# A two-layer decoder trunk on one core: first tile's rows through two PSUM banks, a tile's closing steps moved to later slots, GELU taken of the place matrix

## What is computed

```python
def peer_ffn(xn, w_q, sub_keys, u_tab, v_tab):            # 16384 experts, 8 heads, top 16 of each
    q = (xt @ w_q).reshape(n_tok, 8, 2, 128)
    scores = einsum('thcd,ckd->thck', q, sub_keys)
    top_s, top_i = top_k(scores, 16)                      # then top 16 of the 16 x 16 sums
    gate = softmax(sel_s)                                 # 128 experts and gates for each token
    act = gelu(einsum('td,tkd->tk', xb, u_tab[eb]))
    out = einsum('tk,tkd->td', gb * act, v_tab[eb])
```

## Time and profile before

| | |
|---|---|
| median of 3 executions | 3154.34 us |
| the profiled execution, device time | 3158.17 us |
| its span, first to last instruction | 3156.4 us |
| time outside the span | 1.8 us |
| busy: PE, VectorE, ScalarE, POOL | 2147.1, 2199.8, 1549.0, 1155.9 us |
| mean granted TensorE clock | 0.781 of full |
| DMA | 1185.36 MB, mean 376 GB/s |

### The profile page before, as it was taken

How to read it: one execution, slowest core, us unless ns; L and a number is a source line. 1 busy time by engine, 2 the same in 40 slices (tenths; PEclk the granted TensorE clock), 3 DMA queues, 4 the chain that set the end, 5 groups by cost and what they waited for, 6 DMA issues and landing times.

```text
span 3156.4 us, 40113 instructions
## 1 busy us (share of the span) xinstructions
PE 2147.1 (68%) x13768; PEld 1281.2 (41%) x13768; DVE 2199.8 (70%) x6053; ACT 1549.0 (49%) x3986; POOL 1155.9 (37%) x1041
## 2 busy tenths in 40 slices
PE   7878788674457798777855799878675655453334
PEld 6776454340024475555523466545442312120001
DVE  8646888857776777767676657777866666667663
ACT  3514556443334766775433476787543423343332
POOL 0012344334443333434343433433445444334441
PEclk8889888785567899998876799999886866565555
DMA  6228999999999999979999999998999999999995
GB/s 212 67 86 334 419 419 417 396 369 421 421 420 364 419 404 391 403 287 410 419 420 414 377 356 399 384 388 339 421 420 420 420 421 421 421 419 421 421 421 241
DMA packets 182413, 1185.36 MB, mean 376 GB/s; under 512 B 19648, under 2 KB 25792, under 8 KB 50880
## 3 DMA queue, kind: packets, MB, share of 16 engines
q0 software_dynamic: 147456, 1073.81, 83.0%
q1 hardware_dynamic: 34752, 108.98, 9.1%
HBM read 1180.61 MB, written 2.10 MB: 375 GB/s over the span
## 4 chain that ended last, share of the span: by engine, by line
DMA 37%; PE 31%; ACT 16%; DVE 9%; issue 5%; POOL 2%; another core or an unknown queue 1%; ACTq 0%; SPq 0%; POOLq 0%; DVEq 0%
DMA arena<-uv_tab,cols 37%; PE ps L760 7%; PE xps L696 7%; DVE arena L2179 4%; PE ps L696 4%; POOL arena L653 2%; ACT L1415 2%; ACT scr L1427 2%; ACT cols L1420 2%; PE ps L735 2%; PE xps L1118 2%; PE xps L1192 1%; ACT cols L1415 1%; PE xps L1169 1%; PE xps L1189 1%
## 5 line engine op out<-in xcount | busy, mean ns | idle before, releaser
L653 POOL DMA_INDIRECT arena<-uv_tab,cols x1024 | 1151.7, 1125 | 1944.8 <-PE ps L760 1372.2
L2179 DVE CUSTOM_DVE_ANT_0 arena<-arena 128x1024 f32<-128x1024 f32 x1024 | 1249.8, 1222 | 588.6 <-DMA arena<-uv_tab,cols 558.5
L760 PE MATMUL ps<-arena,scr 128*32 128x512 f32 x4096 | 743.3, 806 | 751.8 <-ACT scr L1427 729.2
L1415 ACT ACTIVATE cols<-cols 128x2 f32<-128x2 f32 x512 | 105.2, 206 | 1008.1 <-DVE cols L2179 998.0
L760 PEld LDWEIGHTS ps<-arena,scr 128*32 128x32 f32 x4096 | 92.7, 123 | 1121.8 <-ACT scr L1427 1036.8
L696 PE MATMUL xps<-arena,wring 128*128 128x256 f32 x1600 | 393.6, 396 | 15.8 <-ACT arena L1628 8.3
L696 PEld LDWEIGHTS xps<-arena,wring 128*128 128x128 f32 x1600 | 304.1, 197 | 105.8 <-issue 43.1
L1427 ACT ACTIVATE scr<-sel,cols 128x32 f32<-128x32 f32 x1024 | 275.3, 316 | 48.4 <-ACT cols L1420 1.9
L696 PE MATMUL ps<-arena,wring 128*128 128x256 f32 x1152 | 292.2, 411 | 6.6 <-DVE arena L1807 4.1
L696 PEld LDWEIGHTS ps<-arena,wring 128*128 128x128 f32 x1152 | 233.7, 207 | 90.7 <-issue 46.2
L1420 ACT ACTIVATE cols<-cols 128x1 f32<-128x1 f32 x1024 | 247.9, 289 | 20.5
(11 more groups left out here) (447 smaller groups left out, 2911.9 us busy)
## 6 DMA issues: line engine op xcount, KB each, us to landing
wring<-wall SPq DMA_DIRECT2D x176, 512.0 KB
arena<-uv_tab,cols POOLq DMA_INDIRECT x1024
arena<-wall SPq DMA_DIRECT2D x16, 512.0 KB, 7.5
h<-xT SPq DMA_DIRECT2D x2, 1024.0 KB, 11.3
arena<-glu_w SPq DMA_DIRECT2D x2, 1024.0 KB, 12.7
out<-arena SPq DMA_DIRECT2D x4, 512.0 KB, 21.0
arena<-s_b SPq DMA_DIRECT2D x1, 512.0 KB, 9.1
arena<-s_bt SPq DMA_DIRECT2D x1, 512.0 KB, 9.8
```

Of the source, the lines that this page charges most:

```text
L653: pool.indirect_dma_start(out=whole_row(at), out_offset=None, in_=uv_tab, in_offset=bass.IndirectOffsetOnAxis(ap=ids[g % 2][:, k:k + 1], a ...
L760: mm = pe.matmul(ps[4 + half][32 * c:32 * c + 32, :], wdiag[:, b % PAIRS, j, :], pair_row(at + j, 1)[:, T * half:T * half + T], start=(g % ...
L1415: mark(act.activation(gelu[g % 2][:, 2 * b:2 * b + 2], dots[g % 2][:, 2 * b:2 * b + 2], ACT.Gelu))
L2179: dve.tensor_tensor_reduce(u, u, xrep[:, block_of(k), :], 1.0, 0.0, ALU.mult, ALU.add, dots[g % 2][:, k:k + 1]).then_inc(s["dot_done"], 1)
```

## The change

Four things are edited.

1. Tile 0's rows have a step of their own, `first_tile_rows`, through banks 0 and 1 in turn in place of the side bank, so PE's step i waits for the copy of step i - 2. PE does six of the eight steps (before: two) ahead of `across(0)`, and ScalarE four of the eight copies (before: two) ahead of `soft(0)`. `u_rows` gets a wait for the last copy, since it writes these banks next. `first_apply(1)` goes from behind dot 0 to behind dot 1.
2. The first round of a later tile: rows 5, 6, 7 go from slots 1, 1.5, 2 to 2, 3.5, 5; the closing steps from 2.5, 3, 4.5 to 6, 7, 8.5 (PE), and from 3, 3.5, 5 to 6.5, 7.5, 9 (ScalarE); `tile_done` from 6 to 9 to 10 to 13; the query of rounds 16, 32 and 48 from 5 to 9.
3. Routing: in these rounds route(r + 2) starts at slot 14 in place of 11, and ScalarE's `soft` of the next head is at slot 5 in place of 3 in the round after.
4. `gelus`: GELU of `place` scaled by the dot (two of 128x32) straight to `wdiag`, then two copies in place scaled by the gate. GELU of a dot into columns, the gate's product there and the spreading go away. The wait for `v_free` moves ahead of the GELU.

```diff
@@ def query_at(gi, q):
-    return 16 * r + (8 if r == 0 else 5 if r % 8 == 0 and r > 0 else 2)
+    return 16 * r + (8 if r == 0 else 9 if r % 8 == 0 and r > 0 else 2)
@@ def rows_at(t, i):
-    return TOPK * PH * t + (-7, -5.5, -4, -2.5, 0.5, 1, 1.5, 2)[i]
+    return TOPK * PH * t + (-7, -5.5, -4, -2.5, 0.5, 2, 3.5, 5)[i]
@@ def side_order():
-    todo = [(-10, "q", 0, -1), (-9, "sc", 0, -1), (-8, "q", 0, -2), (-7.5, "x", 0, 0), (-7.2, "x", 0, 1), (-7, "sc", 0, -2)]
-    todo += [(-6 + 0.1 * i, "x", 0, i) for i in range(2, 8)] + [(4.5, "q", 0, 0), (6.7, "sc", 0, 0)]
+    todo = [(-10, "q", 0, -1), (-9, "sc", 0, -1), (-8, "q", 0, -2), (-7, "sc", 0, -2), (4.5, "q", 0, 0), (6.7, "sc", 0, 0)]
...
-        todo += [(TOPK * (PH * t + 8) + (2.5, 3, 4.5)[i], "hy", t, i) for i in range(3)]
+        todo += [(TOPK * (PH * t + 8) + (6, 7, 8.5)[i], "hy", t, i) for i in range(3)]
@@ PE
+            def first_tile_rows(i):
+
+                pe.wait_ge(s["xn_first"], 1)
+                if i >= 2:
+                    pe.wait_ge(s["rows_done"], i - 1)
+                for k in range(4):
+                    for e in range(4):
+                        mm = pe.matmul(ps[i % 2][32 * e:32 * e + 32, tl(k)], xn[:, 4 * (i % 2) + k, 32 * (i // 2):32 * (i // 2) + 32],
+                                       ident[:, :], start=True, stop=True, skip_group_check=True)
+                mm.then_inc(s["rows_mm"], 1)
...
-            for i in range(2):
-                to_rows(0, i)
+            for i in range(6):
+                first_tile_rows(i)
             across(0)
             first_scores(1)
-            for i in range(2, 8):
-                to_rows(0, i)
+            for i in range(6, 8):
+                first_tile_rows(i)
             first_sum(1)
...
-                    if k in (2.5, 3, 4.5) and done is not None:
-                        finish(done, (2.5, 3, 4.5).index(k))
+                    if k in (6, 7, 8.5) and done is not None:
+                        finish(done, (6, 7, 8.5).index(k))
@@ ScalarE
+            def first_tile_rows(i):
+
+                act.wait_ge(s["rows_mm"], i + 1)
+                act.activation(xrep[:, i // 2, T * (i % 2):T * (i % 2) + T], ps[i % 2][:, :],
+                               ACT.Copy).then_inc(s["rows_done"], 1)
...
-                mark(act.activation(gelu[g % 2][:, 2 * b:2 * b + 2], dots[g % 2][:, 2 * b:2 * b + 2], ACT.Gelu))
+                if 8 * g + b >= PAIRS:
+                    act.wait_ge(s["v_free"], 2 * (8 * g + b - PAIRS) + 2)
                 if b == 0:
                     act.wait_ge(s["gate_found"], g + 1)
+                for n in two:
+                    m = act.activation(wdiag[:, b % PAIRS, n % 2, :], place, ACT.Gelu, scale=dots[g % 2][:, n:n + 1])
+                mark(m)
                 settled()
                 for n in two:
-                    m = act.activation(gelu[g % 2][:, n:n + 1], gelu[g % 2][:, n:n + 1], ACT.Copy,
+                    m = act.activation(wdiag[:, b % PAIRS, n % 2, :], wdiag[:, b % PAIRS, n % 2, :], ACT.Copy,
                                        scale=gate[g % 2][:, n:n + 1])
-                mark(m)
-                if 8 * g + b >= PAIRS:
-                    act.wait_ge(s["v_free"], 2 * (8 * g + b - PAIRS) + 2)
-                settled()
-                for n in two:
-                    m = act.activation(wdiag[:, b % PAIRS, n % 2, :], place, ACT.Copy, scale=gelu[g % 2][:, n:n + 1])
                 m.then_inc(s["w_ready"], 1)
...
-            for i in range(2):
-                to_rows(0, i)
+            for i in range(4):
+                first_tile_rows(i)
             soft(0)
             first_scores(1)
-            for i in range(2, 8):
-                to_rows(0, i)
+            for i in range(4, 8):
+                first_tile_rows(i)
             first_norm(1)
...
-                    if k == 3 and r + 1 < ROUNDS:
+                    if k == (5 if r % PH == 1 else 3) and r + 1 < ROUNDS:
                         soft(r + 1)
...
-                    if k in (3, 3.5, 5) and done is not None:
-                        finish(done, (3, 3.5, 5).index(k))
+                    if k in (6.5, 7.5, 9) and done is not None:
+                        finish(done, (6.5, 7.5, 9).index(k))
@@ VectorE
             def tile_done(t):
-                yield 6
+                yield 10
...
-                    if r == 0 and k == 0:
+                    if r == 0 and k == 1:
                         first_apply(1)
...
-                    if k == (14 if r == 0 else 11 if r % PH == 0 else ROUTE_SLOT):
+                    if k == (14 if r % PH == 0 else ROUTE_SLOT):
                         nxt = route(r + 2) if r + 2 < ROUNDS else iter(())
```

More of the change, by code:

```diff
@@ L514, in trunk @@
         dots = [rcol(384 + 16 * i, TOPK) for i in range(2)]
-        gelu = [rcol(416 + 16 * i, TOPK) for i in range(2)]
         def score_at(t, q):
@@ L531, in trunk @@
             "g_sq", "g_sum", "g_root", "mix1_ready", "out_added", "hsq_ready", "hsum", "h_root", "xn_ready",
-            "first_w", "first_mm", "xn_first", "q_first",
+            "first_w", "first_mm", "xn_first", "q_first", "rows_mm", "rows_done",
             "q_mm", "m_mm", "o_mm", "side_mm", "side_done", "na_ready",
@@ L723, in scores @@
                 mm.then_inc(s["side_mm"], 1)
+            def first_tile_rows(i):
[7 more added lines that the diff above has]
+                mm.then_inc(s["rows_mm"], 1)
             def to_rows(t, i):
                 side_free(("x", t, i))
-                if t == 0:
-                    pe.wait_ge(s["xn_first"], 1)
-                else:
-                    pe.wait_ge(s["xn_ready"], t // 2 + 1)
+                pe.wait_ge(s["xn_ready"], t // 2 + 1)
                 at = P * (t % 2) + 32 * (i // 2)
@@ L793, in u_rows @@
                         pe.wait_ge(s["u_ready"], i)
+                    if g and i == 0:
+                        pe.wait_ge(s["rows_done"], 8)
                     if g and i >= 2:
@@ L1396, in scores @@
                 m.then_inc(s["side_done"], 1)
+            def first_tile_rows(i):
+                act.wait_ge(s["rows_mm"], i + 1)
+                act.activation(xrep[:, i // 2, T * (i % 2):T * (i % 2) + T], ps[i % 2][:, :],
+                               ACT.Copy).then_inc(s["rows_done"], 1)
             def to_rows(t, i):
                 act.wait_ge(s["side_mm"], SIDE_MM["x", t, i])
-                if t:
-                    act.wait_ge(s["dot_done"], PH * TOPK * t - TOPK + 8 * (i // 4) + 7 + i // 2 % 2)
+                act.wait_ge(s["dot_done"], PH * TOPK * t - TOPK + 8 * (i // 4) + 7 + i // 2 % 2)
                 act.activation(xrep[:, i // 2, T * (i % 2):T * (i % 2) + T], side[:, :],
@@ L2174, in dot @@
                 at = g * TOPK + k
-                if g % PH == 0 and k % 8 < 2:
+                if g == 0 and k % 8 < 2:
+                    dve.wait_ge(s["rows_done"], 2 * block_of(k) + 2)
+                elif g % PH == 0 and k % 8 < 2:
                     dve.wait_ge(s["side_done"], SIDE["x", g // PH, 2 * block_of(k) + 1] + 1)
@@ L2194, in tile_done @@
                     if i < 3:
-                        yield 7 + i
+                        yield 11 + i
                 m.then_inc(s["tile_normed"], 1)
```

## The result

| | before | after |
|---|---|---|
| median, us | 3155.22 | 3109.36 |
| lowest to highest, us | 3153.1 to 3158.18 | 3107.85 to 3114.19 |
| span of the profiled execution, us | 3156.4 | 3106.1 |
| busy PE, VectorE, ScalarE, us | 2147.1, 2199.8, 1549.0 | 2128.0, 2205.4, 1466.2 |

The change takes 0.9857 of the time before (95% interval 0.984 to 0.9874), that is 45 us less, and 50.3 on the two profiled spans (the profiled execution of the kernel before took 3158.17 us, 3 us above its median). The forecast was 34 us less.

A forecast was written before the change was run, and what follows sets the result against it. The prediction took DMA transfers, plus stretches where the DMA engines lack work, to bound the kernel. Its terms 10 + 20 + 0 + 4 = 34 us took the median from 3154.3 to 3120, range 3096 to 3143.

The forecast's parts named there:

- What bounds it: Whole kernel: time is the transfers' time plus stretches where DMA engines lack work, at the start and tile changes.
- Part 1: Start, tile 0's rows through two banks: the DMA gap at 240 to 256 us shrinks, 10 us, ends 5 and 13.
- one pause left: Start, ScalarE's row copies: of two pauses only the longer remains, gather near 245, worth 10 us.
- both pauses: Start: both ScalarE pauses remain and PE's clock halves between them; apply near 239.3, gather near 249.5, worth 6.5 us.
- Part 2: Tile changes: moved row and closing steps shrink POOL's waits toward 5 us; 20 us, ends 3 and 31.
- The upper end of 31: Five tile changes: POOL's waits all shrink toward a pair's nominal 5 us, saving 31 us.
- Part 3: Routing, seven rounds: later route puts 2.9 us more in one VectorE piece; priced at nothing, 20 us if cover is gone.
- The slower rival: VectorE's longer piece in slot 5 delays dots and empties the ring after seven tile changes; 3180 us, chance 0.06.
- Part 4: Gelus: each pair's chain 0.2 us shorter, at most 27 us over 135 pairs; 4 us taken, ends 0 and 14.
- Only move their gap: Tile changes: PE is busy, so pairs come late a few slots further on; 3140 us, chance 0.17.
- Everything in full: No pause at the start, 13; tile changes 31; shorter pair 8 to 10; 3101 us, chance 0.18.
- Doesn't do what it says: Start: the first gap stays, held up by the first gathers whatever the bank; 3151 us, chance 0.04.

The follow-up runs named there:

- The rows alone: Kernel before with only row steps 5 to 7 of later tiles moved, to slots 2, 3.5 and 4; ratio 1.0021, 6.6 us more.
- the slots as a whole: Kernel before with only the new places of rows, closing steps, query, soft, tile_done and route; 3132.4 us, ratio 0.9929.
- The lengthened pairs: Changed kernel with further 128x1 ScalarE copies per pair, inside its chain or behind it; with two copies, ratio 0.9942 inside, 0.9915 behind.
- four copies: Changed kernel with four further 128x1 copies per pair: behind the chain 34.9 us more; inside, with two further handovers, 34 us more than that.
- part 4 alone: Kernel before with only the new gelus, including the moved v_free wait; 3141.8 us, ratio 0.9957, 13.6 us less.

## Why the prediction was right

The time lies in the range, 11 us on the better side of the forecast, and the kernel is faster as expected. By its steps:

**What bounds it: right.** No gain stands in rounds 2 to 8 or 46 to 63, where the DMA share is 1.01 (table of gathers). At the start and the tile changes, 9.4 and 30 us went.

**Part 1, 10 taken, 8.2 measured.** The step that failed is "one pause left": both remain, 4.25 and 5.31 us, and with the gathers held both go. The first gather comes 1.4 us later than before, where 0.5 was reckoned; 0.8 of this was there before the change's first instruction (PE's L984 at 199.12, L976 of the kernel before at 198.31), so the rest is as reckoned. 9.4 us of gap less 1.4 is 8.0. The apply at 238.29 and the gather at 247.58 lie near the "both pauses" end (239.3 and 249.5). The other end came out too, on the chip without pauses: its apply starts at 228.75 us and its ninth gather at 239.08, where 228.5 and 239 were reckoned. So the working was right and the choice between its two ends was a guess about something that changes from chip to chip. The Trainium skill ("Runtime: NRT & Kernel Launch", Instruction fetch mechanics) says that crossing a block is mostly hidden, and by it the prediction had 6.5, as near to the 8.2 as its 10. As far as it shows fetches, the trace agrees that the pauses are none: neither ends on an instruction packet, and the packet like that of the earlier trace rows comes only at 233.20 here, 1.9 us after the last copy has begun. But they don't belong to the copies either, as the prediction went on to say: the copies wait for PE's signal.

**Part 2, 20 taken, 22.4 measured.** Right in size and mechanism. POOL's longest waits in the five pairs of rounds are 8.3, 7.1, 9.5, 6.3 and 8.8 us, below 9 at four of them as foretold. The upper end of 31 wasn't reached: the change between tiles 2 and 3 keeps (1.01 - 0.86) x 103 = 15.5 us of idle DMA of (1.01 - 0.82) x 109 = 20.7. The prediction had named its dip at 1375 to 1395 as out of reach and PE's 43 of 50 busy us there. What the prediction hadn't seen is that its two halves live on each other. The rows alone make the kernel slower.

**Part 3, 0 taken.** The slower rival doesn't show: none of the five pairs of rounds, which hold rounds 9, 17, 25, 33 and 41, got longer or emptier, and the slots as a whole give what part 2 promised. It wasn't run alone, so a cost of a few us inside the 22.4 stays possible.

**Part 4, 4 taken, 13.6 measured (8 to 19).** This is the term that was mis-sized. The saving per pair was right, 0.19 us against 0.2. Wrong was the reason for cutting its ceiling of 27 to 4, that PE's order and not the chain is the limit where the DMA isn't full. The lengthened pairs price the loop: 22.7 us for 0.5 us, so 0.19 us would be 8.6 by that slope, at the low end of the interval. Half of such a price is the chain's own and half is what ScalarE's work costs wherever it stands (four copies: 69 inside, 35 behind), and part 4 took away both, 0.19 us of chain and (1549.0 - 1466.2) / 512 = 0.16 us of work for each pair. That the gain lies above 8.6 may be the interval; it isn't settled. The doses were given to the kernel after and part 4 alone to the kernel before, and a price that rises with the length would make the last 0.19 us worth less than 8.6, so the curve doesn't explain the difference. As the total lies only 1.4 us above the range's lower end of 3108, this one term nearly carried the time out of the range. The places fit: the gelus' gain and the doses' cost fall in rounds 18 to 44, between the tile changes too, where the prediction had counted almost nothing. The Trainium skill's figure ("ScalarE: Activation LUTs", What ACT_TABLE_LOAD costs) gave a saving of 0.13 us a pair and 3 us in all; the rows' 0.19 differs, and the sum by it errs in the same way as mine.

**The rivals.** "Only move their gap" is refuted for the change as a whole (30 us less at the tile changes) and true for its rows alone. "Everything in full" is half true: the shorter pair gave more than its 8 to 10, the tile changes and the start didn't come in full. 3109 lies about halfway between the forecast of 3120 and this rival's 3101. "Doesn't do what it says" is refuted by the start, where 9.4 us of the gap are gone.

## What to carry to other kernels

In a kernel bound by transfers, compare the start of the same transfer in two traces: the difference by round tells which stage each microsecond came from, which neither busy shares nor the longest waits do. A latency of 0.2 us on a loop that feeds the transfers is worth more than the visible gaps suggest when the DMA share is a few per cent short over a long stretch; price it with a dose inside the loop and the same dose behind it. When steps are moved out of a crowd, move all that they would meet, and try each half alone. And before a pause is put down to a cause, look for it in a profile of the same kernel on another chip, and at the time at which the awaited semaphore rose.

## What the runs showed of the hardware

- Under the first gathers (DMA share 0.99 over 222 to 240 us) PE's signal for two steps rose 3.5 and 5.5 us after their last recorded matmul, ScalarE's copies idled 4.25 and 5.31 us with the releaser "remote", and PE's small matmuls came in groups of four or five, 0.3 to 1.0 us apart. With the gathers held back for 3.4 us, and with the gathers in flight on another chip (DMA share 1.00 over the same stretch), the copies idled 0.79 and 0.27 us and PE's 64 matmuls ran in one piece.
- With 1024 more instructions on ScalarE the queue q14 carried 99 packets in place of 91, with 2048 more 107, of 8 KB each.
- A 128x32 ACTIVATE with a pointer operand took 315 ns with Gelu and 313 with Copy; the 128x1 copies 279 behind the chain and 287 inside it. The size hardly matters here, the count does.
- The same kernel before took 3156, 3141 and 3143 us on three chips, while the ratio of the kernel after was 0.9857 and 0.9855 on two of them.
